# The experts' first 58 slabs in wide products, with the two halves of each sum added by GpSimd

## The chip, the cores and the metric

The kernel runs on one core of a Trainium2 chip. The core has five engines that run at the same time, each with a queue of its own: TensorE (PE, with its weight loads shown as PEld), VectorE (DVE), ScalarE (ACT), GpSimd (POOL) and SyncE (SP), which issues transfers. They wait for each other through semaphores. The metric is the device time of one execution in microseconds, lower is better. The kernel before takes 2132.78 us (median of 3 runs, 2130.16 to 2136.34).

## The reference

A decoder trunk of 2 layers over 256 tokens of width 1024. Each layer has a mixer, a cross-attention and an expert network. The change touches the last one, whose core is:

```
def peer_ffn(h, w_pq, sub_keys, u_experts, v_experts):
    q = (xb @ w_pq).reshape(PEER_BLOCK, P_HEADS, 2, P_HALF)
    sc = jnp.einsum('thpc,hpkc->thpk', q, sub_keys)
    sv, si = lax.top_k(sc, TOPK)
    ...                                   # the best 16 of 16 x 16 pairs, their experts eid, weights g
    a = jax.nn.gelu(jnp.einsum('thkd,td->thk', ue, xb), approximate=False)
    return jnp.einsum('thk,thkd->td', g * a, ve)
```

There are 128 x 128 experts. The kernel gathers nothing: it multiplies all 16384 rows of `u_experts` with all tokens, takes the gelu, multiplies by a gate that is zero except for the chosen experts, and multiplies by all of `v_experts`. All is float32.

## The kernel before, in words

All weights are one stream of *slabs*, 128 partitions x 1024 float32 (512 KB), 340 a layer. A slab goes through four slots (`RING` = 4) in the same way everywhere:

- SP loads slab n+4 into `raw` of slot n % 4 when DVE is done with slab n (`next_slab`, wait on `lo_ready`).
- ACT copies `raw` to `w_hi`, rounded to the type that TensorE multiplies fast. It may do so for slab n+4 once TensorE has finished slab n, which used the slot (`slab_done`), and the load has landed (`raw_loaded`).
- DVE subtracts `w_hi` from `raw`, which gives the rest `w_lo` (`lo_part`).
- TensorE multiplies. The operand is split in the same way into `act_hi` and `act_lo`, and a product is hi x hi + lo x hi + hi x lo.

There are two ways to do the product. `slab_product` (L1283 to L1292) issues, for each of 8 chunks of 128, three products of 256 columns into one sum in PSUM: 24 instructions a slab. `wide_product` (L1294 to L1301) keeps `act_hi` and `act_lo` beside each other in `act_2` and multiplies `w_hi` with both by one instruction of 512 columns, and `w_lo` with `act_hi` by one of 256: 16 instructions a slab. It leaves two sums in the two halves of a PSUM bank, and somebody has to add them.

The experts' 128 slabs of `u_experts` (U slabs) come in this order in each layer:

- U slabs 0 to 57 by `slab_product`. ACT takes the gelu straight from PSUM into one of two `h_out` slots (`gelu_out`, L684 to L692) and then converts the next slab. SP stores the slot to DRAM (`store_h`). Meanwhile DVE finds the top 16 of the scores and decodes them, with a `lo_part` put in between by a table of costs (`spend`, `next_lo`).
- Before U slab 58 TensorE turns the decoded indices around (wait on `decoded`), and DVE builds operands for the gate from them.
- U slabs 58 to 123 by `wide_product`, in the part that also builds the gate: ACT copies one half out (`half_of`), DVE adds the other (`add_u`), ACT takes the gelu (`gelu_of`).
- U slabs 124 to 127 by `slab_product`.

Then 128 slabs of `v_experts` follow, where GpSimd multiplies the stored gelus by the gate.

Around the change, the order of the queues matters. SP's loop over U slabs is `next_slab(n)`, `store_h(n-2)`, `next_slab(n+1)`, `store_h(n-1)`, and so on, so that the load of slab s+7 is issued after the store of slab s, which waits for the gelu of slab s (`act_evac`). TensorE starts U slab n when `lo_ready` tells that `w_lo` of slab n is there and `act_evac` that the gelu of slab n-4 is done, which frees its bank.

Of the kernel before, what the change touches and what calls it, by code (L numbers as in the profile page):

```python
# [26 lines left out]
ALU = mybir.AluOpType  # L27
ACT = mybir.ActivationFunctionType
# [3 lines left out]
P = 128  # L32
D = 1024
KB = D // P
T = 256
# [17 lines left out]
U_SLABS = V_SLABS = 128  # L53
# [8 lines left out]
U_AT = PQ_AT + PQ_SLABS  # L62
V_AT = U_AT + U_SLABS
SLABS = V_AT + V_SLABS
# [3 lines left out]
RING = 4  # L68
# [4 lines left out]
U_EV = PQ_EV + PQ_SLABS  # L73
ACT_EVS = U_EV + U_SLABS
# [23 lines left out]
HOT_AT = 60  # L98
RET_AT = 58
# [5 lines left out]
H_SLOTS = 2  # L105
# [34 lines left out]
def trunk(nc, x, mem, slabs, params, sub_keys, out):  # L140
    ctx = ExitStack()
    with ctx:
# [5 lines left out]
        def at(name, offset, shape, dt=FP32):  # L148
            return nc.alloc_sbuf_tensor_at(name, shape, dt, offset=offset)
# [24 lines left out]
        hot_row = at("hot_row", x_at + 2048, [P, 2, PARTS, P, 2], BF16)  # L174
        h_out = at("h_out", x_at + 6144, [P, H_SLOTS, T])
        early_hi = at("early_hi", x_at, [P, EARLY, T], F32R)
        early_in = at("early_in", x_at + EARLY * T * 4, [P, EARLY, T])
# [107 lines left out]
        def sem(name):  # L285
            return ctx.enter_context(nc.semaphore(name))
# [7 lines left out]
        act_evac, dve_evac = sem("act_evac"), sem("dve_evac")  # L294
        half_out, u_half, u_sum = sem("half_out"), sem("u_half"), sem("u_sum")
        x_loaded = [sem(f"x_loaded{m}") for m in range(X_PARTS)]
        x_ffn, par_first, par_loaded = sem("x_ffn"), sem("par_first"), sem("par_loaded")
# [138 lines left out]
        def _(pool):  # L436
# [12 lines left out]
            def scale(dst, count, evacs, xns):  # L449

                pool.wait_ge(xn_ready, xns)
                pool.wait_ge(act_evac, evacs)
                for i in range(count):
                    last = nc.gpsimd.tensor_tensor(dst[:, i, :], dst[:, i, :], rstd_pre[:], ALU.mult)
                last.then_inc(scaled, 1)
# [19 lines left out]
            for layer in range(DEPTH):  # L475
# [9 lines left out]
                sum_chunks(layer, SUM_XO, OUT_SLABS)  # L485
                scale(qpT, 2 * RING, layer * ACT_EVS + PQ_EV + 2 * RING + RING, layer * (2 * XN_USES) + 2 * XN_INDEX[USE_FFN] + 1)

                pool.wait_ge(act_ready, (layer + 1) * (2 * USES))
# [30 lines left out]
        def _(act):  # L519
# [73 lines left out]
            for layer in range(DEPTH):  # L593
# [89 lines left out]
                def gelu_out(at0, g, j):  # L683
# [8 lines left out]
                                         ACT.Copy).then_inc(hi_ready, 1)  # L692

                def experts(at0, slabs_n):
                    with act.Fori(0, slabs_n // RING) as g:
                        for j in range(RING):
                            gelu_out(at0, g, j)

# [9 lines left out]
                settle(act)  # L708
                experts(0, RING)
                scores_out(1, scores1)  # L710
# [20 lines left out]
                for j in range(RING - 2):  # L731
                    gelu_out(HOT_AT - RING, 0, j)
                half_of(HOT_AT - RING, 0, RING - 2)
# [82 lines left out]
        def _(dve):  # L816
# [103 lines left out]
            for layer in range(DEPTH):  # L920
# [252 lines left out]
                step.link(nc.vector.tensor_tensor(g_parts[:, :, 2, :], g_rest[:], g_parts[:, :, 1, :], ALU.subtract))  # L1173
                dve.wait_ge(x_parked, layer * 16 + 16)
                for j in range(2):
                    lo_part(layer, U_AT + HOT_AT, 0, j)
# [106 lines left out]
        def _(pe):  # L1283
# [87 lines left out]
            for layer in range(DEPTH):  # L1371
# [244 lines left out]
                scores(0)  # L1616
                project(layer, U_AT, RING, act_evac, U_EV, ACT_EVS)
                pe.wait_ge(sc_evac, layer * TB + 1)
                scores(1)
                project(layer, U_AT + RING, RET_AT // RING * RING - RING, act_evac, U_EV + RING, ACT_EVS)  # L1620
                at = RET_AT // RING * RING
                group(layer, U_AT + at, U_EV + at, slots=range(RET_AT % RING))
                pe.wait_ge(decoded, layer + 1)
# [118 lines left out]
```

## Time and profile before

| what | value |
|---|---|
| median of 3 runs | 2132.78 us |
| the profiled execution | 2134.49 us |
| its span | 2132.4 us |
| TensorE busy | 2106.7 us, 99% |
| VectorE busy | 1639.7 us, 77% |
| ScalarE busy | 1142.0 us, 54% |
| GpSimd busy | 341.1 us, 16% |
| mean granted TensorE clock | 0.994 |
| transfers | 204 GB/s over the span |

The profile is of one execution. Its span is the time between the first and the last instruction that the profiler saw, 2.1 us less than the execution's own time. An engine that is busy 99% of the span is the one to look at first, but the number says only that something ran: matmuls overlap, so that their busy time says nothing of how dense they stand. For that one takes the distance between the starts of things that happen once a slab. In layer 0 the U slabs 0 to 59 run from 296 to 473 us, in layer 1 from 1354 to 1531 us.

### The profile page before, as it was taken

Reading aid. Unit: us, or ns where it says so; the run is one execution under the profiler, and the core shown is the slowest. Engines: PE = TensorE matmul, PEld = TensorE weight load, DVE = VectorE, ACT = ScalarE, POOL = GpSimd, SP = SyncE. Lnnn points to the kernel's source line nnn. Section 1 sums busy time; section 2 is a strip of 40 time slices with the busy share of each in tenths; the row PEclk is TensorE's granted clock in tenths of the full one; section 3 lists DMA queues with packets and bytes.
Section 4 is the critical chain, followed back from the end, with each engine's and each line's share of the span. In section 5 each row is a group of like instructions: output and inputs, shape, how many; then the busy total and the mean of one; then the engine's idle time right before and its main releaser. Section 6 shows DMA issues by size and latency. Waiting matters only on the chain. (4 is left out here: it accounts for less than half of the span.)

```text
span 2132.4 us, 43548 instructions
## 1 busy us (share of the span) xinstructions
PE 2106.7 (99%) x13336; PEld 1858.1 (87%) x13336; DVE 1639.7 (77%) x2901; ACT 1142.0 (54%) x1763; POOL 341.1 (16%) x342
## 2 busy tenths in 40 slices
PE   8999999999999999999999999999999999999998
PEld 6898999998888888888878989999988888888886
DVE  7776769989888667777687857699898886666676
ACT  6544544456666554554565445444566665455453
POOL 4010110000000243333330101000000003333332
PEclk9999999999999999999999999999999999999999
DMA  6445557665555877777653454676655558777773
GB/s 226 130 159 168 168 194 231 226 206 187 184 187 187 272 240 242 241 240 243 209 178 119 164 180 164 199 230 225 202 190 184 184 188 282 244 238 242 241 240 129
DMA packets 174222, 435.19 MB, mean 204 GB/s; under 512 B 19504, under 2 KB 85040, under 8 KB 173136
## 3 DMA queue, kind: packets, MB, share of 16 engines
q1 hardware_dynamic: 173520, 430.06, 61.6%
q0 software_dynamic: 640, 4.32, 0.6%
q8 instruction: 37, 0.61, 0.1%
q14 instruction: 25, 0.20, 0.0%
HBM read 397.60 MB, written 36.70 MB: 204 GB/s over the span
## 5 line engine op out<-in xcount | busy, mean ns | idle before, releaser
L822 DVE TENSOR_TENSOR w_lo<-raw,w_hi 128x1024 fp32r<-128x1024 f32 x674 | 835.3, 1240 | 295.5 <-ACT w_hi L766 194.8
L1299 PE MATMUL ps<-act,w_hi 128*128 128x512 f32 x1632 | 598.7, 407 | 0.0
L1659 PE MATMUL ps<-w_hi,act 128*128 128x512 f32 x1936 | 597.1, 389 | 0.9 <-DVE act L1217 0.9
L1300 PE MATMUL ps<-act,w_lo 128*128 128x256 f32 x1632 | 457.0, 280 | 0.0
L1290 PE MATMUL ps<-act,w_hi 128*128 128x256 f32 x2432 | 439.8, 283 | 0.1
L766 ACT ACTIVATE w_hi<-raw 128x1024 fp32r<-128x1024 f32 x248 | 263.1, 1061 | 323.2 <-PE ps L1659 313.4
L1659 PEld LDWEIGHTS ps<-w_hi,act 128*128 128x128 f32 x1936 | 363.5, 188 | 77.3 <-DVE act L1217 1.7
L1290 PEld LDWEIGHTS ps<-act,w_hi 128*128 128x128 f32 x2432 | 380.0, 192 | 0.5 <-DVE act L892 0.4
L1659 PE MATMUL ps<-w_lo,act 128*128 128x512 f32 x968 | 376.6, 389 | 0.0
L1299 PEld LDWEIGHTS ps<-act,w_hi 128*128 128x128 f32 x1632 | 309.4, 190 | 68.0 <-issue 2.7
L1290 PE MATMUL ps<-act,w_lo 128*128 128x256 f32 x1216 | 344.1, 283 | 0.0
L1300 PEld LDWEIGHTS ps<-act,w_lo 128*128 128x128 f32 x1632 | 310.5, 190 | 0.1
L501 POOL TENSOR_TENSOR h_in<-h_in,gate 128x256 f32<-128x256 f32 x250 | 237.5, 951 | 445.8 <-DMA h_in<-h_park 445.8
L1290 PEld LDWEIGHTS ps<-act,w_lo 128*128 128x128 f32 x1216 | 233.4, 192 | 0.0
L1659 PEld LDWEIGHTS ps<-w_lo,act 128*128 128x128 f32 x968 | 181.8, 188 | 37.3
L529 ACT ACTIVATE w_hi<-raw 128x1024 fp32r<-128x1024 f32 x168 | 176.7, 1054 | 69.5 <-PE ps L1290 44.8
L1217 DVE TENSOR_TENSOR act<-h_in,act 128x256 fp32r<-128x256 f32 x250 | 189.7, 759 | 6.3 <-ACT act L754 6.3
L687 ACT ACTIVATE h_out<-ps 128x256 f32<-128x256 f32 x124 | 47.6, 384 | 172.9 <-PE ps L1290 168.6
L723 ACT ACTIVATE w_hi<-raw 128x1024 fp32r<-128x1024 f32 x132 | 138.9, 1052 | 0.0
L493 POOL DMA_DIRECT2D par<-params x2 | 1.2, 594 | 834.3 <-DVE hot_row L1194 834.3
L1194 DVE TENSOR_TENSOR hot_row<-row_is,g_parts 128x768 bf16<-128x768 bf16 x256 | 130.5, 551 | 0.0
L691 ACT ACTIVATE w_hi<-raw 128x1024 fp32r<-128x1024 f32 x124 | 130.3, 1051 | 0.0
(269 smaller groups left out, 2277.0 us busy)
## 6 DMA issues: line engine op xcount, KB each, us to landing
raw<-slabs SPq DMA_DIRECT2D x680, 512.0 KB, 3.9
h_park<-h_out SPq DMA_DIRECT2D x256, 128.0 KB, 1.7
h_in<-h_park SPq DMA_DIRECT2D x250, 128.0 KB, 3.9
memT<-mem POOLq DMA_DIRECT2D x2, 1024.0 KB, 6.0
skT<-sub_keys POOLq DMA_DIRECT2D x2, 1024.0 KB, 7.9
x_park<-xT SPq DMA_DIRECT2D x2, 1024.0 KB, 5.6
xT<-x_park SPq DMA_DIRECT2D x2, 1024.0 KB, 7.3
xT<-x SPq DMA_DIRECT2D x4, 256.0 KB, 5.4
```

Of the source, the lines that this page charges most:

```text
L501: nc.gpsimd.tensor_tensor(h[:, n:n + 1, :], h[:, n:n + 1, :], gate[:, ds(g * RING + j, 1), :], ALU.mult).then_inc(gated_ready, 1)
L529: nc.scalar.activation(w_hi[:, j].rearrange("p k c -> p (k c)"), raw[:, j, :], ACT.Copy).then_inc(hi_ready, 1)
L691: nc.scalar.activation(w_hi[:, j].rearrange("p k c -> p (k c)"), raw[:, j, :], ACT.Copy).then_inc(hi_ready, 1)
L723: nc.scalar.activation(w_hi[:, j].rearrange("p k c -> p (k c)"), raw[:, j, :], ACT.Copy).then_inc(hi_ready, 1)
L766: nc.scalar.activation(w_hi[:, j].rearrange("p k c -> p (k c)"), raw[:, j, :], ACT.Copy).then_inc(hi_ready, 1)
L822: nc.vector.tensor_tensor(w_lo[:, j].rearrange("p k c -> p (k c)"), raw[:, j, :], w_hi[:, j].rearrange("p k c -> p (k c)").bitcast(FP32), ...
L1194: last = nc.vector.tensor_tensor(hot_row[:, e], row_is[:, e:e + 1].to_broadcast([P, PARTS, P, 2]), of_pick[:, PARTS * e:PARTS * e + PARTS] ...
L1217: nc.vector.tensor_tensor(lo[:, j:j + 1, :], h[:, j:j + 1, :], hi[:, j:j + 1, :].bitcast(FP32), ALU.subtract).then_inc(ga_ready, 1)
L1290: last = nc.tensor.matmul(ps[:, j, 0:T], w[:, j, k, :], a[:, k, :], start=(k == 0 and i == 0), stop=(k == KB - 1 and i == 2))
L1299: nc.tensor.matmul(ps[:, j, :], w_hi[:, j, k, :], a[:, :, k, :], start=(k == 0), stop=False)
L1300: last = nc.tensor.matmul(ps[:, j, 0:T], w_lo[:, j, k, :], a[:, 0, k, :], start=False, stop=(k == KB - 1))
L1659: last = nc.tensor.matmul(ps[:, 2 * b + half, :], a[:, j, b * P:(b + 1) * P], w[:, j, 4 * half:4 * half + 4, :].rearrange("p k c -> p (k c)"),
```

## The change

U slabs 0 to 57 of each layer use `wide_product`. ACT copies the whole bank, both halves, 512 columns, into a new buffer `u_both` of two slots (`both_out`); GpSimd adds the second half to the first (`add_u` in GpSimd's queue); ACT takes the gelu of the sum from SBUF into `h_out` (`added_gelu`). ACT's order is: copy of slab n, conversion of slab n+4, gelu of slab n-1. SP's queue keeps its order. `u_both` lies in memory that the gate's operands use later, so DVE waits for all 58 gelus before its first use of it.

```diff
+        u_both = at("u_both", x_at, [P, H_SLOTS, 2, T])
...
+                def add_u(g, j):
+                    both = u_both[:, j % H_SLOTS]
+                    pool.wait_ge(u_copied, layer * WIDE_AT + g * RING + j + 1)
+                    nc.gpsimd.tensor_tensor(both[:, 0, :], both[:, 0, :], both[:, 1, :], ALU.add).then_inc(u_added, 1)
...
+                def both_out(at0, g, j):
+
+                    act.wait_ge(slab_done, layer * SLABS + U_AT + at0 + g * RING + j + 1)
+                    act.wait_ge(act_evac, layer * ACT_EVS + U_EV + RING + at0 + g * RING + j - 1)
+                    nc.scalar.activation(u_both[:, j % H_SLOTS].rearrange("p i t -> p (i t)"), ps[:, j, :],
+                                         ACT.Copy).then_inc(u_copied, 1)
+
+                    act.wait_ge(raw_loaded[j], (layer * (SLABS // RING) + ((U_AT + at0) // RING + 2) + g) * 16)
+                    nc.scalar.activation(w_hi[:, j].rearrange("p k c -> p (k c)"), raw[:, j, :],
+                                         ACT.Copy).then_inc(hi_ready, 1)
+
+                def added_gelu(at0, g, j):
+
+                    act.wait_ge(u_added, layer * WIDE_AT + at0 + g * RING + (j + 1))
+                    act.wait_ge(h_stored[j % H_SLOTS], (layer * (U_SLABS // H_SLOTS) + at0 // 2 + g * 2 + j // 2) * 16 + 16)
+                    nc.scalar.activation(h_out[:, j % H_SLOTS, :], u_both[:, j % H_SLOTS, 0, :],
+                                         ACT.Gelu).then_inc(act_evac, 1)
+
                 def experts(at0, slabs_n):
                     with act.Fori(0, slabs_n // RING) as g:
                         for j in range(RING):
-                            gelu_out(at0, g, j)
+                            both_out(at0, g, j)
+                            added_gelu(at0, g, j - 1)
...
                 for j in range(RING - 2):
-                    gelu_out(HOT_AT - RING, 0, j)
+                    both_out(HOT_AT - RING, 0, j)
+                    added_gelu(HOT_AT - RING, 0, j - 1)
+                added_gelu(HOT_AT - RING, 0, RING - 3)
                 half_of(HOT_AT - RING, 0, RING - 2)
...
                 dve.wait_ge(x_parked, layer * 16 + 16)
+                dve.wait_ge(act_evac, layer * ACT_EVS + U_EV + RING + WIDE_AT)
...
-                project(layer, U_AT, RING, act_evac, U_EV, ACT_EVS)
+                project(layer, U_AT, RING, act_evac, U_EV, ACT_EVS, True)
...
-                project(layer, U_AT + RING, RET_AT // RING * RING - RING, act_evac, U_EV + RING, ACT_EVS)
+                project(layer, U_AT + RING, RET_AT // RING * RING - RING, act_evac, U_EV + RING, ACT_EVS, True)
                 at = RET_AT // RING * RING
-                group(layer, U_AT + at, U_EV + at, slots=range(RET_AT % RING))
+                wide_group(layer, U_AT + at, U_EV + at, slots=range(RET_AT % RING))
```

ScalarE's queue where U slab 48 begins, before (L713 is the exponential of the gate's weights; L687 the gelu, L691 the conversion; what an instruction waits for stands in brackets):

```order
L713 ACT_TABLE_LOAD
L713 ACTIVATE g_exp<-g_exp 128x256 [waits fin_ready]
L695 UNCONDITIONAL_BRANCH
L695 ISA
L686 ISA [waits slab_done]
L687 ACT_TABLE_LOAD
L687 ACTIVATE h_out<-ps 128x256 [waits h_stored0]
L690 ISA
L691 ACTIVATE w_hi<-raw 128x1024 [waits raw_loaded0]
```

The same place after (L748 is the exponential; L711 the copy of both halves, L715 the conversion, L722 the gelu):

```order
L748 ACT_TABLE_LOAD
L748 ACTIVATE g_exp<-g_exp 128x256 [waits fin_ready]
L726 UNCONDITIONAL_BRANCH
L726 ISA
L710 REGISTER_ALU [waits slab_done]
L711 ACT_TABLE_LOAD
L711 ACTIVATE u_both<-ps 128x512 [waits act_evac]
L714 ISA
L715 ACTIVATE w_hi<-raw 128x1024 [waits raw_loaded0]
L720 REGISTER_ALU
L721 ISA [waits u_added]
L722 ACT_TABLE_LOAD
```

The gelu moved from in front of the conversion to behind it and belongs to the slab before, and the loop, which runs twice from here, has two table loads in each round instead of one.

VectorE's queue where it turns from decoding to the gate, before (L1168 to L1173 prepare the gate's factors, L822 are the `lo_part` of U slabs 60 and 61):

```order
L1168 CAST pick_at<-ps 128x512 [waits ret_mm]
L1170 CAST g_parts<-ps 128x128x2
L1171 TENSOR_TENSOR g_rest<-ps,g_parts 128x256 [waits dve_step]
L1172 CAST g_parts<-g_rest 128x128x2 [waits dve_step]
L1173 TENSOR_TENSOR g_parts<-g_rest,g_parts 128x128x2 [waits dve_step]
L822 TENSOR_TENSOR w_lo<-raw,w_hi 128x1024 [waits hi_ready,x_parked,dve_step]
L822 TENSOR_TENSOR w_lo<-raw,w_hi 128x1024 [waits hi_ready]
```

And after, with the line numbers of the changed kernel (L859 is `lo_part`):

```order
L1210 TENSOR_TENSOR g_parts<-g_rest,g_parts 128x128x2 [waits dve_step]
L859 TENSOR_TENSOR w_lo<-raw,w_hi 128x1024 [waits act_evac,hi_ready,x_parked,dve_step]
L859 TENSOR_TENSOR w_lo<-raw,w_hi 128x1024 [waits hi_ready]
L1242 UNCONDITIONAL_BRANCH
L1242 ISA
```

Nothing moved there, but the first `lo_part` waits for ACT's 58th gelu as well.

## Rows read from the trace of the kernel before

**Rows 1.** The page, part 1: busy time and share of each engine.
```profile
PE 2106.7 (99%) x13336; PEld 1858.1 (87%) x13336; DVE 1639.7 (77%) x2901; ACT 1142.0 (54%) x1763; POOL 341.1 (16%) x342
```
**Rows 2.** Busy time by stretch: start:end, length, engines, granted clock, DMA share, GB/s.
```profile
340.00:380.00 40.00, 40.00 (x335) 40.00 (x335) 36.35 (x135) 18.63 (x28) 0.00 (x0) 1.00 0.69 228
```
**Rows 3.** Timeline of ACT: start, length, instruction, idle before; wide slabs, then narrow ones.
```profile
281.37 0.38 ACT L542 ACTIVATE qpT<-ps 128x256 f32 x1 [1.49 <-PE ps L1300]
...
292.68 0.38 ACT L542 ACTIVATE qpT<-ps 128x256 f32 x1 [1.50 <-PE ps L1300]
...
340.03 0.38 ACT L687 ACTIVATE h_out<-ps 128x256 f32<-128x256 f32 x1 [1.45 <-PE ps L1290]
...
374.59 0.38 ACT L687 ACTIVATE h_out<-ps 128x256 f32<-128x256 f32 x1 [1.45 <-PE ps L1290]
```
**Rows 4.** Waits, 300 to 460 us: who, for whom, total us, times, longest.
```profile
ACT h_out L687 <- PE ps L1290: 76.9, 51, 1.7
...
SPq L333 <- ACT h_out L687: 82.5, 52, 5.2
```
**Rows 5.** Timeline of SP: the store of a gelu (L359), the next load (L340).
```profile
343.63 0.35 SPq L359 DMA_DIRECT2D h_park<-h_out  x1
344.24 0.34 SPq L340 DMA_DIRECT2D raw<-slabs  x1
...
349.41 0.35 SPq L359 DMA_DIRECT2D h_park<-h_out  x1
350.12 0.34 SPq L340 DMA_DIRECT2D raw<-slabs  x1
352.17 0.35 SPq L359 DMA_DIRECT2D h_park<-h_out  x1
353.21 0.34 SPq L340 DMA_DIRECT2D raw<-slabs  x1
```
**Rows 6.** Timelines of ACT and DVE: a gelu, a conversion, its `lo_part`.
```profile
343.00 0.38 ACT L687 ACTIVATE h_out<-ps 128x256 f32<-128x256 f32 x1 [1.65 <-PE ps L1290]
343.28 1.05 ACT L691 ACTIVATE w_hi<-raw 128x1024 fp32r<-128x1024 f32 x1
...
344.37 1.23 DVE L822 TENSOR_TENSOR w_lo<-raw,w_hi 128x1024 fp32r<-128x1024 f32 x1 [0.18 <-ACT w_hi L691]
```
**Rows 7.** Tile `raw`: loads, issue to landing; at 320 to 420, then 800 to 1000 us.
```profile
DMA to landing us min/median/max: 3.1/3.5/4.5
...
DMA to landing us min/median/max: 4.1/4.4/5.0
```
**Rows 8.** ACT: 512 columns from PSUM, a gelu from SBUF, an instruction behind a conversion.
```profile
L743 ACT ACTIVATE gate<-ps x7: 587/588/591, 476.2 to 497.1; 128x512 f32 x7
...
L729 ACT ACTIVATE h_out<-h_out x132: 403/419/420, 474.7 to 1759.9; 128x256 f32<-128x256 f32 x132
...
800.93 1.06 ACT L766 ACTIVATE w_hi<-raw 128x1024 fp32r<-128x1024 f32 x1 [1.35 <-PE ps L1659]
801.90 0.40 ACT L754 ACTIVATE act<-h_in 128x256 fp32r<-128x256 f32 x1
```
**Rows 9.** Timeline of ACT: a table load in the loop.
```profile
452.43 1.28 ACT L687 ACT_TABLE_LOAD   x1 [1.63 <-PE ps L1290]
```
**Rows 10.** Timelines of ACT and DVE where U slab 57 ends: last gelu, DVE's turn.
```profile
466.75 0.39 ACT L687 ACTIVATE h_out<-ps 128x256 f32<-128x256 f32 x1 [1.55 <-PE ps L1290]
...
467.40 0.69 DVE L1168 CAST pick_at<-ps 128x512 bf16<-128x512 f32 x1 [3.15 <-PE ps L1626]
...
469.70 2.36 DVE L822 TENSOR_TENSOR w_lo<-raw,w_hi 128x1024 fp32r<-128x1024 f32 x2
```
**Rows 11.** Timelines of POOL and DVE in the second expert product.
```profile
854.71 0.81 POOL L501 TENSOR_TENSOR h_in<-h_in,gate 128x256 f32<-128x256 f32 x1 [1.91 <-DMA h_in<-h_park]
...
854.85 0.96 DVE L1217 TENSOR_TENSOR act<-h_in,act 128x256 fp32r<-128x256 f32 x1
...
876.61 0.42 DVE L1217 TENSOR_TENSOR act<-h_in,act 128x256 fp32r<-128x256 f32 x1
```

More of the change, by code:

```diff
@@ L295, in trunk @@
         half_out, u_half, u_sum = sem("half_out"), sem("u_half"), sem("u_sum")
+        u_copied, u_added = sem("u_copied"), sem("u_added")
         x_loaded = [sem(f"x_loaded{m}") for m in range(X_PARTS)]
@@ L486, in _ @@
                 scale(qpT, 2 * RING, layer * ACT_EVS + PQ_EV + 2 * RING + RING, layer * (2 * XN_USES) + 2 * XN_INDEX[USE_FFN] + 1)
+                def add_u(g, j):
+                    both = u_both[:, j % H_SLOTS]
+                    pool.wait_ge(u_copied, layer * WIDE_AT + g * RING + j + 1)
+                    nc.gpsimd.tensor_tensor(both[:, 0, :], both[:, 0, :], both[:, 1, :], ALU.add).then_inc(u_added, 1)
+                with pool.Fori(0, WIDE_AT // RING) as g:
+                    for j in range(RING):
+                        add_u(g, j)
+                for j in range(WIDE_AT % RING):
+                    add_u(WIDE_AT // RING, j)
                 pool.wait_ge(act_ready, (layer + 1) * (2 * USES))
@@ L708, in _ @@
                 settle(act)
-                experts(0, RING)
+                for j in range(RING):
+                    both_out(0, 0, j)
+                    if j:
+                        added_gelu(0, 0, j - 1)
                 scores_out(1, scores1)
```

## The prediction, made before the changed kernel ran

> **What bounds the kernel now.** I read the page first: TensorE is busy for 99% of the span [rows 1], so only its queue can shorten the time, and any wait put into it costs in full. Next I took the busy times of a quiet stretch in the part that changes [rows 2]: TensorE 40.00 of 40 us at clock 1.00, DVE 36.35, ACT 18.63, GpSimd idle. The list of waits [rows 4] says the same from the other side: ACT waits for TensorE slab after slab (76.9 us between 300 and 460 us), and SP waits for ACT's gelu, 82.5 us in 52 waits. That SP wait is harmless here, but the change makes the gelu later, so I keep it in mind.
>
> How much time a slab takes I read from the starts of the instruction that ACT does once a slab. Narrow: (374.59 - 340.03) / 12 = 2.880 us. Wide, in the query projection, with the same operand `act_2`: (292.68 - 281.37) / 4 = 2.8275 us [rows 3]. So 16 instructions in place of 24 save only 0.0525 us, 2%.
>
> **What the change removes.** 58 slabs x 0.0525 = 3.05 us a layer, 6.1 us in all. This is the whole possible gain, since TensorE does not wait now: 0.29%. [...] The rows say 2.880 and 2.8275, and the sum goes by them.
>
> **What it adds, and whether that is hidden.** ACT's work for a slab was a gelu and a conversion. Now it is a copy of 512 columns (0.59 us, as L743), a conversion, and a gelu from SBUF (0.42 us, as L729) [rows 8]. An instruction behind a conversion starts 0.97 us after the conversion's start [rows 8], and a conversion behind a copy about 0.5 us after it (a gelu of 0.38 us is followed after 0.28 [rows 6]). Together 0.5 + 0.97 + 0.32 = 1.8 us of 2.83: hidden by TensorE. GpSimd's add of 256 columns is of the kind of L501, 0.81 us in the row at hand [rows 11]; it has more than 2 us until its gelu: hidden, 0. `lo_part` comes 0.2 us later; it ends at 345.60 and TensorE wants it at 343.00 + 3 x 2.88 = 351.6 [rows 6], 6 us in hand: 0.
>
> The critical edit is the move of the gelu behind the *next* slab's copy and behind the conversion that waits for a load. SP issues the load of slab s+7 after the store of slab s. Before, that gelu came right after TensorE finished slab s. Now the gelu of slab s comes after the conversion of slab s+5, and that needs the load of slab s+5. So the load of s+7 depends on the load of s+5: a loop that must go round in the time of two slabs, 2 x 2.8275 = 5.655 us. Its length, step by step:
> - conversion's start to gelu's start 0.97, gelu 0.42 [rows 8];
> - gelu's end to SP's store: 343.63 - 343.38 = 0.25 [rows 5, 6];
> - store to load: 0.61, 0.71 and 1.04 in the three pairs shown, and a further 0.61 in the pair at 346 us that is left out; mean 0.74 [rows 5];
> - load to landing 3.5 [rows 7];
> - waking ACT 0.05 (DVE starts 344.37 - 344.33 = 0.04 after the conversion that it waits for [rows 6]).
>
> Sum 5.93 us, 0.275 more than two slabs. Before, the load issued at 344.24 [rows 5] was wanted at 343.00 + 3 x 2.88 + 0.28 = 351.9 and landed at 347.7, 4.2 us early. In the new order nothing is left at the start either: from the end of slab s+1 the gelu of s ends at 0.05 + 0.5 + 0.97 + 0.42 = 1.94, the load is issued at 2.93 and lands at 6.43; ACT wants it at 5.655 + 0.55 = 6.2. So the lag starts at once and grows by 0.275 each round. The first load so bound is that of U slab 11, the last that matters is slab 61: 25 rounds, 6.9 us.
>
> Table loads come on top. One takes 1.28 us and stands behind the wait for TensorE, on ACT's path [rows 9]. In the loop over slabs 48 to 55 each of two rounds now has one before the copy and one before the gelu. The two before a gelu are in the loop of the loads: 2.57 us. The exponential with its own load and the first one before a copy (1.28 + 0.42 + 1.28 = 2.98) meets ACT's spare time of 2.95 - 1.8 = 1.15 and adds 1.8. The lag of even slabs grows by 4.4; an odd slab only has to stand behind its neighbour in ACT's queue, 1.15 less: 3.2 at slab 61. Lag there 6.9 + 3.2 = 10.1 us.
>
> What does the lag cost? First TensorE: slab n needs the gelu of n-4, which without lag is ready 5.655 - 1.94 = 3.7 us early, so once the lag is above that TensorE waits for ACT in each slab. Second, DVE's new wait. It reaches `lo_part` of slab 60 at 469.70, 2.95 us after the gelu of slab 57 began [rows 10]. The 58th gelu now ends 0.5 + 0.97 + 0.32 + 0.42 = 2.2 us after its copy begins, plus the lag: the first 0.75 us are free. Behind this wait stand the `lo_part` of 60 and 61 and the gate's first operands, for which TensorE waits. These two costs are the same lag seen at two places, not two terms: what counts is when DVE passes the wait. A layer: -3.05 + 10.1 - 0.75 = +6.3 us. Two layers +12.6.
>
> The part behind is unchanged and starts that much later. On the profiled execution's 2134.49 us this makes 2147.1; that execution was 1.7 us above the median of the runs, so on the median 2132.78 it is **2145.4 us**.
>
> **Bounds.** The landing is the term on which all hangs: 25 rounds x 2 layers, so 0.1 us in it is 5 us. At the shortest landing, 3.1, the loop is 5.53 and needs no more than two slabs: only the table loads remain, -3.05 + 3.2 - 0.75 = -0.6 a layer, 2131.6. At 3.75, between the 3.5 here and the 4.4 that loads take beside more traffic [rows 7], the excess is 0.525 a round: -3.05 + 13.1 + 3.2 - 0.75 = 12.5 a layer, 2157.8. At 4.4 it would be 2190; there the transfers compete with other reads, which is not the case here.
>
> **The rivals.**
> A. The gain comes: the loads keep up and the table loads fall into waits. Then -6.1, 2126.7. For it: four slots, and loads that land after 3.1 us [rows 7]. Against it: every number of the loop would have to be at its smallest.
> B. The loads keep up but the table loads are felt at DVE's new wait: 2131.6, as above.
> C. DVE becomes the bound by GpSimd. In the second expert product DVE's L1217 takes 0.96 us when a GpSimd instruction began before it and 0.42 alone [rows 11]: 0.54 us lost. If each of the 58 adds did that to a DVE instruction, DVE would need 36.35 / 40 x 2.88 + 0.54 = 3.16 us a slab against 2.88 now: 58 x 0.28 = 16 us less the 6 in hand, 10 a layer, and 2153. The Trainium skill has the rule, "SBUF — State Buffer", section "SBUF: two separate sides": the port pair that the two share is an exclusive lock, taken by a VectorE instruction with two SBUF inputs or by GpSimd's, whoever comes first. By that rule the trace agrees in [rows 11]. Against a full price here: the add starts 0.6 us after TensorE's slab end, when DVE is mostly in its maximum searches with one input, and `lo_part` starts later, after the conversion.
> D. The loop is longer than I think (transfers slower, another delay in ACT's queue): 2158 and above.
>
> **How the numbers follow.** Chances: the forecast 0.58, A 0.06, B 0.18, C 0.10, D 0.08. The forecast's own range is 2138 to 2155. The range for 8 in 10 takes in B below and part of D above: 2130 to 2159. A measurement of this kernel tells about 0.3%, 6.4 us, from no change: faster means below 2126.4, only half of A; the same up to 2139.2, B, the rest of A and the lowest edge of the forecast. Faster 0.03, same 0.27, slower 0.70.
>
> **What the new profile would show.** ACT's conversions in the stage wait for a DMA (`raw`), where now they wait for TensorE; SP's wait for the gelu stays; the starts of TensorE's slabs are 2.83 us apart up to about U slab 30, then near 2.96, with TensorE waiting for ACT's gelu; between slabs 59 and 60 TensorE stands for several us and DVE waits for the gelu L722. DVE's `lo_part` stays at 1.22 us. The prediction is wrong if conversions do not wait for loads, if slab starts stay at 2.83 to the end, or if DVE's instructions get longer beside GpSimd's.

## The result, and the profile after

| | median us | runs | lowest to highest |
|---|---|---|---|
| before | 2132.85 | 7 | 2130.16 to 2136.59 |
| after | 2151.77 | 7 | 2144.07 to 2156.98 |

The ratio is 1.0082, with an interval of 1.0066 to 1.0098: slower, by 18.9 us between the medians. The profiled execution took 2151.99 us, its span is 2150.3, 17.9 above the span before.

The page of the changed kernel, part 1, beside [rows 1]:
```profile
PE 2107.7 (98%) x12408; PEld 1810.4 (84%) x12408; DVE 1651.7 (77%) x2901; ACT 1219.3 (57%) x1883; POOL 457.9 (21%) x458
```
TensorE issues 928 instructions fewer (58 slabs, 8 each, two layers), and its busy time has not fallen. What it waits for shows in the waits of the changed kernel; the first two rows are TensorE's of 290 to 484 us, the next two those of layer 1 (1345 to 1550), then one of DVE's of 290 to 484 us and, of 300 to 460 us, ACT's and SP's, beside [rows 4]. Columns: engine and line <- who is waited for: total us, times, longest.
```profile
PE ps L1675 <- DVE hot_row L1232: 5.9, 1, 5.9
PE ps L1337 <- ACT h_out L722: 3.2, 1, 3.2
...
PE ps L1337 <- ACT h_out L722: 4.7, 3, 3.0
PE ps L1675 <- DVE hot_row L1232: 4.2, 1, 4.2
...
DVE w_lo L859 <- ACT h_out L722: 4.5, 1, 4.5
...
ACT w_hi L715 <- DMA raw<-slabs: 38.9, 42, 2.7
...
ACT u_both L711 <- PE ps L1338: 6.9, 10, 1.2
...
SPq L335 <- ACT h_out L722: 95.2, 52, 12.1
```
ACT had waited for TensorE, 76.9 us in 51 waits; now it waits for loads, 38.9 us in 42, and TensorE waits for ACT's gelu and, ahead of the gate, for DVE, which stood 4.5 us in its new wait.

The loop of the loads stands in ACT's and SP's timelines (start, length), beside [rows 5, 6]: the conversion of slab 29, the gelu of slab 24, its store, the load of slab 31 and the conversion of slab 31. The conversion of slab 7, at 309.60, already waits for its load: that was issued at 304.61, behind the store of the first gelu, which had a table load ahead of it (302.36), and took 5.0 us to land. TensorE was then busy with the second half of the scores and lost nothing by it. The conversions of slabs 8 to 10 don't wait, that of slab 11, at 322.06, does, and from there on nearly all do.
```profile
309.60 1.06 ACT L715 ACTIVATE w_hi<-raw 128x1024 fp32r<-128x1024 f32 x1 [2.66 <-DMA raw<-slabs]
...
322.06 1.06 ACT L715 ACTIVATE w_hi<-raw 128x1024 fp32r<-128x1024 f32 x1 [0.37 <-DMA raw<-slabs]
...
374.28 1.06 ACT L715 ACTIVATE w_hi<-raw 128x1024 fp32r<-128x1024 f32 x1 [0.97 <-DMA raw<-slabs]
375.25 0.40 ACT L722 ACTIVATE h_out<-u_both 128x256 f32<-128x256 f32 x1
...
379.82 1.06 ACT L715 ACTIVATE w_hi<-raw 128x1024 fp32r<-128x1024 f32 x1 [0.92 <-DMA raw<-slabs]
```
```profile
375.91 0.35 SPq L361 DMA_DIRECT2D h_park<-h_out  x1
376.61 0.34 SPq L342 DMA_DIRECT2D raw<-slabs  x1
```
0.97 to the gelu, 0.40 for it, 0.26 to the store, 0.70 to the load, 3.21 until ACT goes on: 5.54 here, and (379.82 - 322.06) / 10 = 5.78 on average. Loads land as before: 3.1/3.4/4.0 us at 320 to 440, against 3.1/3.5/4.5 [rows 7].

The table loads stand where the prediction had them (ACT's timeline, beside [rows 9]):
```profile
438.84 1.28 ACT L748 ACT_TABLE_LOAD   x1
440.13 0.42 ACT L748 ACTIVATE g_exp<-g_exp 128x256 f32<-128x256 f32 x1
440.57 1.28 ACT L711 ACT_TABLE_LOAD   x1
...
443.42 1.28 ACT L722 ACT_TABLE_LOAD   x1
444.71 0.42 ACT L722 ACTIVATE h_out<-u_both 128x256 f32<-128x256 f32 x1
```
TensorE goes on right after that gelu (its timeline):
```profile
445.18 0.57 PE L1337 MATMUL ps<-act,w_hi 128*128 128x512 f32 x1 [3.21 <-ACT h_out L722]
```
Behind both of its waits in layer 0 it runs at the lower of its two clocks; behind the wait of 3.0 us in layer 1 the clock stays at 1.00. Busy time by stretch (columns as in [rows 2], the clock before the DMA share):
```profile
340.00:380.00 40.00, 40.00 (x233) 34.95 (x232) 36.23 (x134) 27.57 (x43) 13.37 (x14) 1.00 0.69 226
...
440.00:445.00 5.00, 1.98 (x12) 1.46 (x10) 4.50 (x6) 4.93 (x7) 1.02 (x1) 1.00 0.41 129
445.00:449.00 4.00, 3.82 (x13) 3.26 (x14) 3.90 (x7) 2.58 (x5) 2.00 (x2) 0.57 0.54 180
449.00:476.00 27.00, 24.33 (x139) 20.70 (x138) 20.75 (x35) 18.32 (x28) 7.50 (x7) 1.00 0.65 209
476.00:483.00 7.00, 3.58 (x19) 3.30 (x20) 6.18 (x13) 3.11 (x6) 0.00 (x0) 0.51 0.57 181
```
Where the time went I read from the first and last starts of two lines. The scores stand ahead of the 60 slabs; the gate's products (L1637 before, L1675 after) stand in each of 64 rounds. Before, then after, layer 0 and layer 1 each:
```profile
L1612 PEld LDWEIGHTS ps<-skT,qpT x64: 188/192/192, 292.3 to 310.8; 128*128 128x128 f32 x64
L1637 PEld LDWEIGHTS ps<-hot_row,hot_col x768: 95/97/103, 474.4 to 698.0; 128*128 128x128 bf16 x192
...
L1612 PEld LDWEIGHTS ps<-skT,qpT x64: 188/192/193, 1350.2 to 1368.7; 128*128 128x128 f32 x64
L1637 PEld LDWEIGHTS ps<-hot_row,hot_col x768: 95/97/103, 1532.0 to 1755.6; 128*128 128x128 bf16 x192
```
```profile
L1650 PEld LDWEIGHTS ps<-skT,qpT x64: 187/192/193, 291.4 to 309.5; 128*128 128x128 f32 x64
L1675 PEld LDWEIGHTS ps<-hot_row,hot_col x768: 95/97/146, 479.4 to 707.6; 128*128 128x128 bf16 x192
...
L1650 PEld LDWEIGHTS ps<-skT,qpT x64: 187/192/193, 1359.1 to 1377.2; 128*128 128x128 f32 x64
L1675 PEld LDWEIGHTS ps<-hot_row,hot_col x768: 95/97/144, 1544.8 to 1772.8; 128*128 128x128 bf16 x192
```
From the first score to the gate I take off 3.5 us, the first 32 scores, and call the rest the slabs' stage (the other 32 scores, 3.5 us more, stand behind slab 3 and are in it in every kernel); the gate's 63 rounds I call the gate's part. By the same two lines of every kernel below (us, layer 0 / layer 1). Each ratio is to the kernel before as measured beside that run, whose median was 2132.85 us beside the changed kernel, 2137.2 beside the first four experiments (store later, loop written out, own place, wide products alone), 2135.74 beside the next four (gelu first, three edits, small adds, stall) and 2135.91 beside the next three: ratios compare over the whole table, medians only within such a group.

| kernel | slabs' stage | gate's part | ratio to before |
|---|---|---|---|
| before | 178.6 / 178.3 | 223.6 / 223.6 | 1 |
| changed | 184.5 / 182.2 | 228.2 / 228.0 | 1.0082 [1.0066, 1.0098] |
| store later | 176.1 / 175.7 | 228.1 / 223.6 | 0.9974 [0.9957, 0.9990] |
| loop written out | 181.6 / 182.0 | 225.1 / 226.1 | 1.0057 [1.0039, 1.0076] |
| own place | 184.0 / 181.4 | 228.1 / 224.1 | 1.0058 [1.0039, 1.0077] |
| wide products alone | 172.5 / 172.2 | 223.6 / 223.6 | 0.9945 [0.9927, 0.9963] |
| gelu first | 176.9 / 176.7 | 225.2 / 225.2 | 0.9995 [0.9982, 1.0008] |
| three edits | 175.9 / 175.6 | 223.6 / 223.6 | 0.9987 [0.9974, 1.0000] |
| three edits, small adds | 172.5 / 172.1 | 223.6 / 223.6 | 0.9943 [0.9923, 0.9963] |
| before, with a stall | 183.3 / 183.3 | 226.0 / 228.9 | 1.0060 [1.0037, 1.0082] |
| 44 wide slabs | 174.0 / 173.6 | 226.5 / 226.5 | 0.9967 [0.9951, 0.9983] |
| changed, small adds | 184.8 / 182.5 | 228.4 / 225.7 | 1.0078 [1.0057, 1.0098] |
| two edits | 176.1 / 175.8 | 228.0 / 223.6 | 0.9988 [0.9974, 1.0001] |
| before once more | 178.6 / 178.3 | 226.5 / 226.6 | one run |

So of the 17.9 us between the spans 9.8 lie in the slabs' stage, 9.0 in the gate's part, which the change does not touch, and -0.9 in all the rest. (In layer 1 of the kernel with three edits and small adds two weight loads of the scores are missing from the trace, and the start is worked out from the last of them.)

Within the stage the loss comes late. In layer 0 TensorE's slabs stand 2.773 us apart, without a loss, up to about 390 us (slab 33). By 441 us they have lost 1.4 us; then come the stop of 3.2 us ahead of slab 51, 1.7 us at the lower clock behind it, two short stops of 0.9 us together, and the wait ahead of the gate, 5.9 us for 1.5 before. In layer 1 the clock does not fall behind the stop, which is most of the 2.3 us between the layers.

The rest moves by some us from one execution to the next: the first score of layer 0, ahead of which nothing differs, is at 288.5 to 295.3 us over these kernels.

### The profile page after: what moved, and what is told of

Same layout as the page of the kernel before. It is cut to its first block and busy times, and to the rows that moved or that the text cites. A ratio compares the mean times of both kernels' runs of the same rounds, so it can differ in the third digit from the quotient of the medians.

```text
span 2150.3 us, 42314 instructions
## 1 busy us (share of the span) xinstructions
PE 2107.7 (98%) x12408; PEld 1810.4 (84%) x12408; DVE 1651.7 (77%) x2901; ACT 1219.3 (57%) x1883; POOL 457.9 (21%) x458
## 5 line engine op out<-in xcount | busy, mean ns | idle before, releaser
L859 DVE TENSOR_TENSOR w_lo<-raw,w_hi 128x1024 fp32r<-128x1024 f32 x674 | 839.1, 1246 | 299.4 <-ACT w_hi L803 194.5
L1337 PE MATMUL ps<-act,w_hi 128*128 128x512 f32 x2560 | 934.2, 407 | 8.2 <-ACT h_out L722 7.9
L1338 PE MATMUL ps<-act,w_lo 128*128 128x256 f32 x2560 | 720.4, 281 | 0.0
L1337 PEld LDWEIGHTS ps<-act,w_hi 128*128 128x128 f32 x2560 | 485.4, 190 | 124.2 <-ACT h_out L722 11.8
L1338 PEld LDWEIGHTS ps<-act,w_lo 128*128 128x128 f32 x2560 | 487.9, 191 | 0.1
L715 ACT ACTIVATE w_hi<-raw 128x1024 fp32r<-128x1024 f32 x116 | 122.9, 1060 | 84.1 <-DMA raw<-slabs 83.8
L493 POOL TENSOR_TENSOR u_both<-u_both 128x256 f32<-128x256 f32 x116 | 112.8, 973 | 271.3 <-ACT u_both L711 271.3
L1675 PE MATMUL ps<-hot_row,hot_col 128*128 128x128 bf16 x1536 | 111.4, 221 | 10.2 <-DVE hot_row L1232 10.2
L1675 PEld LDWEIGHTS ps<-hot_row,hot_col 128*128 128x128 bf16 x1536 | 89.0, 97 | 32.0 <-issue 21.2
L764 ACT ACTIVATE h_out<-h_out 128x256 f32<-128x256 f32 x132 | 55.2, 418 | 104.7 <-DVE h_out L1240 104.7
L791 ACT ACTIVATE act<-h_in 128x256 fp32r<-128x256 f32 x250 | 100.2, 401 | 13.9 <-POOL h_in L514 13.8
L1328 PE MATMUL ps<-act,w_hi 128*128 128x256 f32 x576 | 104.7, 283 | 0.0
```

The source lines that it names most:

```text
L859: nc.vector.tensor_tensor(w_lo[:, j].rearrange("p k c -> p (k c)"), raw[:, j, :], w_hi[:, j].rearrange("p k c -> p (k c)").bitcast(FP32), ...
L1328: last = nc.tensor.matmul(ps[:, j, 0:T], w[:, j, k, :], a[:, k, :], start=(k == 0 and i == 0), stop=(k == KB - 1 and i == 2))
L1337: nc.tensor.matmul(ps[:, j, :], w_hi[:, j, k, :], a[:, :, k, :], start=(k == 0), stop=False)
L1338: last = nc.tensor.matmul(ps[:, j, 0:T], w_lo[:, j, k, :], a[:, 0, k, :], start=False, stop=(k == KB - 1))
L1675: last = nc.tensor.matmul(ps[:, 4 + s, i * P:(i + 1) * P], hot_col[:, i // 2, :, i % 2], hot_row[:, i // 2, part, :, i % 2], start=(part = ...
```

## The experiments

**The lag.** Theory: the loop over two slabs. First cut it at SP, which issues a store only after the load of slab s+7 (here and below against the changed kernel unless another is named):
```
+BEHIND = 3
-                        store_h(layer, g, (j - H_SLOTS) % RING, j - H_SLOTS)
+                        store_h(layer, g, (j - BEHIND) % RING, j - BEHIND)
```


> The changed kernel, with SP's store of a gelu put one load later: the load of slab s+7 is issued before the store of slab s, so it depends on the load of slab s+4 and not s+5. Theory (the loop load, conversion, gelu, store, load goes round in two slabs and is too long, 5.77 us measured against 2 x 2.773): with three slabs in the loop, 8.3 us, no conversion waits for a load, U slab starts stay 2.77 us apart to slab 47, DVE passes its new wait without standing. The stage from U slab 0 to the gate goes from 184.5 and 182.1 us to about 173 to 175, and the whole to 2125 to 2132. Rival (the table loads, or GpSimd holding up DVE, make the lag): conversions stop waiting for loads but the stage stays above 180 us and the time above 2140.

Measured: 2130.92 us, ratio 0.9974. In the waits of 300 to 460 us ACT waits for TensorE again; its three waits for loads are 1.2 us together:
```profile
ACT u_both L712 <- PE ps L1339: 42.7, 47, 1.2
...
ACT w_hi L716 <- DMA raw<-slabs: 1.2, 3, 0.7
```
The stage is 8.4 and 6.5 us shorter. The order of store and load alone turns the change from slower to slightly faster.

The same loop cut at the other end, in ACT's order:
```
 both_out:  copy of slab n
+           added_gelu(n - 1)
            conversion of slab n+4
-           added_gelu(n - 1)
```


> The changed kernel with ScalarE's order in a round turned: copy of slab n, gelu of slab n-1, then the conversion of slab n+4. The gelu no longer stands behind a conversion that waits for the load of w_hi, and the ring of 6 and SyncE's order are left as they are. Theory (the loop of 5.8 us is load, conversion, copy, gelu, store, load, over two slabs of lag): the loop gets shorter, the waits of the conversions for the load (84 us in both layers together) go below 15 us, a layer's slabs take 174 to 177 us as in the kernel with the earlier store, and the median comes near 2130. Rival (the loads themselves are late, whatever the order): the waits stay at 40 us a layer and the median above 2145.

Measured: 2132.74 us, ratio 0.9995; the stage 7.6 and 5.5 us shorter; conversions wait for loads 5.2 us in 5 waits (290 to 482 us). Both cuts work, so it is the loop and not the load itself that was late.

**The table loads.**
```
-                experts(EXP_AT, HOT_AT - RING - EXP_AT)
+                for at0 in range(EXP_AT, HOT_AT - RING, RING):
+                    for j in range(RING):
+                        both_out(at0, 0, j)
+                        added_gelu(at0, 0, j - 1)
```


> The changed kernel with ACT's loop over U slabs 48 to 55 written out, so that its table loads shrink from six a layer (one of the exponential, two before copies, three before gelus, slab 0's included) to three. Theory (loads bind, table loads add 3 to 4 us a layer at DVE's wait and a drop of TensorE's clock at slab 51): 7 to 10 us less than the changed kernel, 2142 to 2145; conversions still wait for loads, some 40 us a layer. Rival (the table loads fall into ACT's waits for loads and cost nothing): 2150 to 2153.

Measured: 2148.65, ratio 1.0057, whose interval overlaps the changed kernel's; the median lies between the theory's and the rival's. The stage is 2.9 us shorter in layer 0 and 0.2 in layer 1; the prediction had 3.2 a layer. In both layers TensorE's stop ahead of slab 51 shrinks to 1.8 us (3.2 and 3.0 in the changed kernel), and the clock stays at 1.00 behind it. So some 1.7 of the 2.9 us in layer 0 are the fall of the clock that no longer happens; in layer 1, where it had not fallen, the stage gains next to nothing. That the loads cost only beside the lag was tested later, with the other two edits in and the loop kept:

> The changed kernel with two of the three edits: the store after the load of slab s+7, and u_both in a place of its own without VectorE's wait; the rounds of slabs 48 to 55 stay a loop, with its table loads. Theory: the store's edit is what counts, and the table loads cost at most what they add to slabs 48 to 55 beyond a lag of 2: a layer's slabs take 175.5 to 176.5 us, and the time is within 3 us of the kernel with all three. Rival (the written-out rounds matter by themselves, 3.2 us a layer as the prediction had it): 179 us a layer, 6 us above it.

Measured: 2133.00, ratio 0.9988, and the stage 176.1 / 175.8 against 175.9 / 175.6 with all three edits. Without the lag the three further table loads of a layer (six in ACT's timeline of the loop, three where it is written out) cost 0.2 us.

**DVE's new wait.**
```
-        u_both = at("u_both", x_at, [P, H_SLOTS, 2, T])
+        u_both = tmp("u_both", 116, [P, H_SLOTS, 2, T])
-                dve.wait_ge(act_evac, layer * ACT_EVS + U_EV + RING + WIDE_AT)
```


> The changed kernel with u_both in a place of its own that the gate's operands do not use, so that DVE's new wait for the 58th gelu is not needed. Theory (the lag shows at that wait, and the conversion of slab 61 itself is late too): DVE waits only for the conversion of slab 61, about 3.3 us less a layer, TensorE stands 2.6 instead of 5.9 us before the gate and its clock falls for less; 2141 to 2146. Rival (the lag is there anyway at slab 61's load and the wait is no more than its witness): within 2 us of 2152.

Measured: 2148.69, ratio 1.0058, the stage 0.5 and 0.8 us shorter, where the theory had 3.3 a layer. As the prediction said, the wait is the same lag seen at another place: without it TensorE stands 2.9 and 2.0 us ahead of the gate for 5.9 and 4.2, but it still waits for ACT's gelu, 4.0 us in each layer, and its clock falls behind that wait in both layers.

**What wide products are worth.** The kernel before, with `wide_product` for slabs 0 to 57; GELU of the first half of the sum only, the second half left out:
```
-                project(layer, U_AT, RING, act_evac, U_EV, ACT_EVS)
+                project(layer, U_AT, RING, act_evac, U_EV, ACT_EVS, True)
```


> The kernel before with nothing but TensorE's part of the change: wide products for U slabs 0 to 57, ScalarE takes the gelu of the first half straight from PSUM, GpSimd does nothing, the second half (hi x lo) is left out of the sum. It shows what the wide products give by themselves. By the slab starts of the changed kernel where no wait stands (2.773 us against 2.880) 58 x 0.107 = 6.2 us a layer less in this stage. In the gate's part the changed kernel needs 3.586 us a slab where the kernel before needs 3.540, with the same instructions. If that comes from TensorE's own queue (its code is another length and lies elsewhere), it is seen here too: 2132.8 - 12.4 + 5.9 = 2126. If it comes from the other engines (GpSimd, ACT's order, the late stores), the gate's part stays at 3.540 and the time is 2120.

Measured: 2125.53, ratio 0.9945; the stage is 6.1 us shorter in both layers, 0.105 us a slab. ACT's timeline of this kernel gives (374.25 - 340.97) / 12 = 2.773 us a slab; in the query projection of the same trace it is (292.26 - 280.96) / 4 = 2.825, as in [rows 3]:
```profile
280.96 0.39 ACT L542 ACTIVATE qpT<-ps 128x256 f32 x1 [1.50 <-PE ps L1300]
...
292.26 0.38 ACT L542 ACTIVATE qpT<-ps 128x256 f32 x1 [1.49 <-PE ps L1300]
...
340.97 0.39 ACT L687 ACTIVATE h_out<-ps 128x256 f32<-128x256 f32 x1 [1.34 <-PE ps L1300]
...
374.25 0.39 ACT L687 ACTIVATE h_out<-ps 128x256 f32<-128x256 f32 x1 [1.34 <-PE ps L1300]
```
The same code by the same line, at two paces, and they go with the place: in both layers of all fourteen profiles the query projection runs at 2.825 or 2.8275 us a slab, and in the slabs' stage every kernel with wide products runs at 2.773 where no wait stands. The gate's part stays at 223.6 here, so of the two cases of the expectation it is the second; the median lies at the first one's figure only because the kernel before, measured beside it, took 2137.2.

**All three edits**, to see whether that gain is reached:

> The changed kernel with the three edits of the first runs together: the store of a hidden slab after the load of slab s+7, the hot expert's rounds written out (no table loads in a loop), and u_both in a place of its own without VectorE's wait for ScalarE. Theory: each of them left one stall of TensorE ahead of the gate's part, and with all of them gone a layer's slabs take 172.4 to 173.5 us, as with the wide products alone, nothing of TensorE waits over 1 us before the gate, the granted clock stays at 1.0 there, the gate's part is 223.7 in both layers, and the time is within 3 us of that kernel: a ratio to before of 0.993 to 0.996. Rival (GpSimd's additions hold VectorE's conversions up): the slabs stay at 175 us or above in both layers and the ratio stays at 0.997 or more.

Measured: 2130.93, ratio 0.9987. The clock stays at 1.0 ahead of the gate and its part is 223.6, but the stage is 175.9 / 175.6: the expectation failed by 3.4 us a layer, and its rival stood. So GpSimd came back in. Its add alone was cut:
```
-                    nc.gpsimd.tensor_tensor(both[:, 0, :], both[:, 0, :], both[:, 1, :], ALU.add)
+                    nc.gpsimd.tensor_tensor(both[:, 0, 0:8], both[:, 0, 0:8], both[:, 1, 0:8], ALU.add)
```


> The kernel with the three edits together, with GpSimd adding 8 of the 256 columns only (the other 248 columns of the second half are left out of the sum), so that its adds are short while every wait and signal stays. Theory (GpSimd's adds cost nothing): within 2 us of the kernel with the three edits. Rival (its adds of 0.97 us lengthen VectorE's conversions, and these release TensorE): 4 us or more below it, with VectorE's mean for the line of the conversions shorter by over 20 ns.

Measured: 2121.37, ratio 0.9943, 9.6 us less; the stage 172.5 / 172.1, all that wide products give. My theory (the adds cost nothing) was wrong and the rival right in size, but its place is only a small part: `lo_part` is 40 ns shorter in this stretch, 1.0 us in all 25, and does not differ at 300 to 400 us (1220 and 1222 ns). DVE's groups of 400 to 475 us, three edits first, then with small adds (count, busy us, mean ns):
```profile
L863 DVE TENSOR_TENSOR w_lo<-raw,w_hi 128x1024 fp32r<-128x1024 f32 x25 | 31.4, 1260 | 1.1 <-ACT w_hi L716 1.1
L1189 DVE SCALAR_TENSOR_TENSOR pick<-a_at,top_i 128x256 bf16<-128x256 bf16 x16 | 8.5, 583 | 0.0
L1189 DVE SCALAR_TENSOR_TENSOR pick<-b_at,top_i 128x256 bf16<-128x256 bf16 x16 | 7.4, 516 | 0.0
```
```profile
L863 DVE TENSOR_TENSOR w_lo<-raw,w_hi 128x1024 fp32r<-128x1024 f32 x26 | 31.6, 1220 | 2.5 <-ACT w_hi L716 2.5
L1189 DVE SCALAR_TENSOR_TENSOR pick<-b_at,top_i 128x256 bf16<-128x256 bf16 x16 | 5.8, 415 | 0.0
L1189 DVE SCALAR_TENSOR_TENSOR pick<-a_at,top_i 128x256 bf16<-128x256 bf16 x16 | 5.8, 418 | 0.0
```
The 32 two-input operations on `pick` take 15.9 us for 11.6. DVE has no room there (busy 29.87 of the 30 us from 428 to 458, 28.59 with small adds), so what it hands to TensorE comes late: TensorE waits 0.7 us for `lo_part`, 1.1 for the decoded indices and 2.1 ahead of the gate, where with small adds only the last stands, at 1.5. GpSimd's add is held up too (its timeline in the kernel with three edits): 1.54 us here, 0.74 in the median and 0.87 in the mean over 300 to 460 us.
```profile
433.16 1.54 POOL L494 TENSOR_TENSOR u_both<-u_both 128x256 f32<-128x256 f32 x1 [1.48 <-ACT u_both L712]
```
The Trainium skill, "SBUF — State Buffer", section "SBUF: two separate sides", calls the port pair that DVE and GpSimd share an exclusive lock: a DVE instruction with two SBUF inputs and a GpSimd one that reads SBUF keep each other out, and whichever starts first holds the pair to its end. The trace agrees: both inputs of these operations lie in SBUF, and they take 583 ns for 418.

Is it the cause in the changed kernel as well? The same cut there:

> The changed kernel itself with GpSimd adding 8 of the 256 columns (the other 248 columns of the second half are left out of the sum). Theory: most of its 182 to 184.5 us a layer is ScalarE's loop of conversion, gelu, store and load, and GpSimd's adds carry part of that loop (0.97 us less in each wait of a gelu) and of VectorE's bf16 operations: 176 to 181 a layer, 2130 to 2145 in all. Rival 1 (the adds cost nothing, as the prediction counted them: a slab's add is over long before its gelu): 182 us a layer and more, 2150. Rival 2 (the adds are the whole loss): 172.4 a layer and 2121.

Measured: 2151.19, ratio 1.0078, the stage 184.8 / 182.5. No: beside the lag the lock is hidden, and the theory of this run fell. It does bite in the changed kernel too: over 400 to 475 us the operations on `pick` take 480 and 508 ns there, and 414 and 416 with small adds. They cost nothing because ACT is later still. The prediction's rival C is thus false for the change as made, and once the lag is gone it is true in kind, at 3.4 us a layer and not 10.

**The gate's part.** It grew by 4.6 and 4.4 us, without a changed instruction. First TensorE's first round there (timelines: changed, then before): 5.20 us for 3.53.
```profile
479.42 1.46 PE L1675 MATMUL ps<-hot_row,hot_col 128*128 128x128 bf16 x12 [5.95 <-DVE hot_row L1232]
484.62 0.86 PE L1675 MATMUL ps<-hot_row,hot_col 128*128 128x128 bf16 x12
```
```profile
474.41 0.86 PE L1637 MATMUL ps<-hot_row,hot_col 128*128 128x128 bf16 x12 [1.50 <-DVE hot_row L1194]
477.94 0.86 PE L1637 MATMUL ps<-hot_row,hot_col 128*128 128x128 bf16 x12
```
In layer 1 the first round is 5.01 us. Then the other 2.9. Theory: both follow from the wait. In the kernel before:
```
+                for _ in range(4):
+                    step.link(nc.vector.tensor_tensor(pick[:, 0:8], pick[:, 0:8], pick[:, 8:16], ALU.add))
                 dve.wait_ge(x_parked, layer * 16 + 16)
```


> The kernel before, with four additions of 1.2 us each on the gate's picked columns in VectorE's order just before it waits for the parked x: nothing of the change is in it, and TensorE stands about 4.9 us longer ahead of the gate's part, in each layer. Theory (a wait of TensorE of some us is enough to lower its clock and to leave it at the slower of two paces for the part that follows): the granted clock falls below 0.7 behind the wait, the first slab of the gate's part takes about 5.2 us for 3.54, the slabs behind it 3.587 us, and the whole is longer by 4.9 + 1.7 + 3 us a layer, some 19 us. Rival (the pace goes with the changed code): the slabs stay at 3.540 us and the whole is longer by 10 to 13 us.

Measured: 2149.60, ratio 1.0060 (13.9 us). The wait is 6.2 us in layer 0, the clock falls behind it, and the first round is 5.91 us:
```profile
480.65 1.46 PE L1639 MATMUL ps<-hot_row,hot_col 128*128 128x128 bf16 x12 [6.18 <-DVE hot_row L1196]
...
486.56 0.86 PE L1639 MATMUL ps<-hot_row,hot_col 128*128 128x128 bf16 x12
```
But the gate's part is 226.0 in one layer and 228.9 in the other: the clock's 2.4 us came in both, the slower pace (63 rounds at 3.587 for 3.540, 2.9 us) in one. Half of the theory holds. A wait need not be so long: in the kernels "store later" and "two edits" TensorE stands 2.1 us ahead of the gate in layer 0, and the first round takes 5.11 and 5.10 us (granted clock 0.54 at 470 to 473 us in the first of them); with all three edits it also stands 2.1 us, and the round takes 3.54 at 1.00. That is why the gate's part of these two is 228.1 and 228.0 in layer 0: 1.6 of the clock and 2.9 of the pace. What decides between them is not shown.

A version without adds beside `pick`, the best that these runs point to, spoke on the pace as well:
```
+N_WIDE = 44
-                experts(RING, EXP_AT - RING)
+                experts(RING, N_WIDE - RING)
+                added_gelu(N_WIDE, 0, -1)
+                for j in range(RING):
+                    gelu_out(N_WIDE, 0, j)
```
(slabs 44 to 57 with `slab_product` and `gelu_out`, as before the change, the three edits in.)

> The kernel with the three edits together, but with wide products and GpSimd's adds for slabs 0 to 43 only; slabs 44 to 57 as in the kernel before. Theory (the 7 us between the three edits and the same with small adds are VectorE's 32 bf16 operations on pick, which GpSimd's adds hold up, at 428 to 458 us): no add stands beside them, their mean is back at 415 to 420 ns, the waits of TensorE before the gate are 1.5 us as before, and a layer's slabs take 172.4 + 14 x 0.107 = 173.9 us in both layers for 175.9 and 175.5; 2 to 5 us less than the three edits. Rival (the adds cost the same anywhere): over 175.5 a layer and no gain.

Measured: 2130.28 (2118.95 to 2133.68), ratio 0.9967, faster than before and than the changed kernel; the stage 174.0 / 173.6, as expected; DVE's `pick` at 415 and 417 ns. Its ratio lies 0.2% below that of the three edits, with intervals that overlap. Yet both layers ran the gate's part at the slower pace, with TensorE's one wait ahead of it 1.5 us and the clock at 1.0. So the slower pace needs no stall. The last run asked whether it needs a change at all:

> The kernel before once more, unchanged, for one more profile. Its own executions lie between 2129 and 2141 us, and the first profile shows both layers' gate parts at 3.540 us a slab, 223.7 us each. Theory now (the two paces of TensorE are a lot that each execution draws for each stretch, whatever the kernel, since the kernel with wide products for 44 slabs shows 3.587 in both layers with no wait over 1.5 us before them): with a chance of about a half one layer at least shows 226.6 us here. Rival (the kernel before is always at the faster pace in this part): both again at 223.7. One profile that shows 223.7 twice leaves both standing.

Measured: 2140.63 us, span 2138.6. The first and last starts (layer 0, then 1):
```profile
L1637 PEld LDWEIGHTS ps<-hot_row,hot_col x768: 96/97/100, 474.6 to 701.1; 128*128 128x128 bf16 x192
L1637 PEld LDWEIGHTS ps<-hot_row,hot_col x768: 96/97/100, 1534.6 to 1761.2; 128*128 128x128 bf16 x192
```
226.5 and 226.6, with the stage equal to the first profile's to 0.1 us. The kernel before has both paces too; 5.9 of the 6.2 us between its two spans are this. So single profiles can't show it as a cost of the change: one execution has it, another has not. Whether the changed kernel meets it more often its seven times (2144.07 to 2156.98) don't tell.

## Why the prediction was right, and where it was not

Slower was right, and so was the mechanism: the loop through load, conversion, gelu, store and load, the table loads, the one late gelu at DVE's wait. Cutting the loop at either end turned the time back to that of the kernel before or better. Forecast 2145.4, measured 2151.77; 6.4 us short. That the number came so near is in part luck, as the terms show:

- *The gain, 3.05 us a layer: mis-sized.* The wide slab was read from the query projection, 2.8275 us. In the slabs' stage the same line takes 2.773: 6.1 a layer (wide products alone). The gain was twice the forecast's.
- *The loop, 5.93 us against 5.655.* Measured 5.78 against 2 x 2.773 = 5.55. Both terms were 0.1 to 0.15 too large, and the excess, 0.23 for 0.275 a round, came out near.
- *The first load that is late is that of slab 11.* It is the first of those that stay late (322.06). That of slab 7 was late before it, by 2.66 us, behind the first gelu's table load, which the forecast left out; it cost TensorE nothing.
- *Slab starts near 2.96 us apart from slab 30.* They stayed at 2.773 to about slab 33 and then lost only 1.4 us up to slab 50. The lag showed as two stops, ahead of slab 51 and ahead of the gate, and hardly as a slower pace.
- *Table loads, 3.2 us a layer.* 2.9 in layer 0, 1.7 of it by the clock, and 0.2 in layer 1; 0.2 without the lag.
- *The stage as a whole, +6.3 a layer.* +5.9 and +3.9, 9.8 for 12.6. Its losses over the wide products alone were 12.0 and 10.0; the forecast's were 9.35. The gain was 3.05 too small, the loss 2.65 and 0.65 too small; the errors nearly cancelled in layer 0 and in part in layer 1. This is luck: the sum hid two errors.
- *"The part behind is unchanged": this step failed.* A TensorE that stood 5.9 and 4.2 us went on at the lower clock: 1.7 us in the first round of layer 0 (5.20 for 3.53), and 1.5 in layer 1 (5.01 for 3.54). That is 3 us that the change causes. The clock was in none of the forecast's terms, and it cost 1.7 us more within the stage, behind the stop ahead of slab 51. The other 5.9 in the profile are the pace, which the kernel before has as well.
- *Rival C.* One of the forecast's own signs of being wrong did come: DVE's instructions got longer beside GpSimd's, `lo_part` to 1299 ns on average (1220 before) and the operations on `pick` to 480 and 508 (416 and 417) over 400 to 475 us. The run with small adds shows that it cost the changed kernel nothing. Against the rival I said that DVE would mostly be in one-input searches. For the maximum searches that holds; in the decoding behind them the 32 operations on `pick` have two inputs, and there the lock bites. It cost nothing only because the lag was longer.

What of the 18.9 us is shown: 9.8 by the stage, about 3 by the clock behind the gate's wait. The other 6 are as large as the pace of the gate's part and lie within what single executions differ by; they stay open.

## What to carry to other kernels

When an edit moves work behind a wait, follow every store and load that its engine queue orders after it: here one position in SP's order was worth 1.1% and decided the sign. Read the price of a new form from the same part of the program that it will run in, and look ahead for the part behind a stall, where the clock has to come back. An engine that is hidden by today's bottleneck (GpSimd beside DVE) is a cost that waits for the bottleneck to be mended.

## What the runs showed of the hardware

- At full granted clock the same code on TensorE has more than one pace. One difference goes with the place: 2.825 to 2.8275 us a wide slab in the query projection and 2.773 in the slabs' stage (1.9%), in every profile. The other goes with the execution: 3.540 or 3.587 us a gate round (1.3%) in two executions of the kernel before, and from layer to layer within one. Neither waits nor the clock's fall decide this one: the slower pace came without them (44 wide slabs, before once more), and the faster behind them (loop written out, gelu first). What sets either, no run shows.
- After 5.9 and 6.2 us of waiting TensorE took 5.20 and 5.91 us for a round of 3.54, at a granted clock of 0.51 over 476 to 483 us in the changed kernel. After 2.1 us it took 5.11 and 5.10 in two kernels and 3.54 in a third; after 3.2 us in the stage the clock fell (0.57 over 445 to 449 us), and after 3.0 us in layer 1 of the same kernel it did not.
- A GpSimd add beside DVE's two-input bf16 operations stretches both: 583 for 418 ns on average, single ones to 0.96 us, and 1.54 us for an add of 0.74. Maximum searches with one input did not change (283 ns on average in the kernel before and with three edits).
